# Moving three tiles' gates in between expert blocks, in a two-layer decoder step

## The chip, the cores and the metric

The kernel runs on one core of a Trainium2 chip. The metric is the time of one execution on the device, in microseconds (us). TensorE multiplies matrices into PSUM, VectorE and ScalarE work on elements, GpSimd issues the indirect transfers, SyncE issues most others, and 16 DMA engines move the data. The engines run on their own and meet at semaphores.

## The reference

One step of a two-layer decoder over 1024 prompt rows and 8 sample rows, width 1024, all float32. Each layer mixes (convolution, attention, a matrix memory), normalises to `h1`, and then computes what this case is about:

```python
def hier_moe(xf, w_group, b_group, w_expert, b_expert, e_gate, e_up, e_down):
    ...
    top_w, top_i = lax.top_k(jax.nn.softmax(e_in, axis=-1), TOP_K)      # TOP_K = 2 of 32 experts
    ...
    return grouped_experts(xf, expert_idx, top_w, e_gate, e_up, e_down)
# per expert block
        hb = jax.nn.silu(xb @ e_gate[e]) * (xb @ e_up[e])               # 1024 -> 256
        return hb @ e_down[e]                                           # 256 -> 1024
# in hybrid_layer
    ple = jnp.einsum('blp,pd->bld', p, w_pe) * jax.nn.sigmoid(jnp.einsum('bld,de->ble', h1, w_pg))
    out = layer_norm(DN_ALPHA * h1 + moe + ple, ln2_g, ln2_b)
```

## The kernel before

One function, `mix_route_experts`, runs once per layer and holds one instruction list per engine. Its order is written out by hand; nothing plans it. Rows are in 9 tiles of 128: eight of the prompt and tile 8 (`TP`), the sample's, of which 8 rows are real.

**Gates and embeddings.** For each tile, `gates(t)` multiplies `h1` by `w_pg` in two halves of 512 columns (8 chunks, 16 matmul instructions each half), `embeddings(t)` multiplies the turned `p` by `w_pe`. ScalarE takes the sigmoid of the first, VectorE multiplies and adds `ALPHA * h1`, and ScalarE stores the result to `BASE` in HBM; `sig` has two buffers, so tile t waits for the store of tile t-2. Before tile 1 the counting matmuls (L2254, L2255) feed VectorE's routing, which ends in three results: the experts' order (`turn_ready`), the row of each token (`dx_ready`), a table of leftover blocks (`r_ready` 2).

**Experts.** GpSimd scatters the rows of `h1` to `XR`, sorted by expert. The experts are ranked by their number of rows. Rank decides how many units of 32 rows an expert gets, from `TURNS`: one gets 4, 18 get 3, 13 get 2, most rows first. 84 units make 21 blocks (`QUADS`) of 4 units. Four units run side by side in TensorE, each against its own expert's weights. Block q is, on TensorE: `gate_up(q)`, `rows_turned(q + 1)`, `down(q - 1)`, `hidden_turned(q)`. So a block of 3- or 4-unit experts takes one or two new experts, and a block of 2-unit experts always two.

**Weights.** An expert's gate and up (2 MB) and down (1 MB) lie in one of five slots, expert e in slot e % 5. The slots lie over buffers that are dead by then: two in the place of `w_out`, the third over the turned `h1` (hT), the fourth over `w_pg`, the fifth ahead of `w_out`. Slots 0 and 1 are loaded during the gates, slot 2 after tile 5's gate, slots 3 and 4 when the gates, and the base's stores, are through. After that SyncE's list `todo` is sorted by the block that frees each buffer: gate and up after `gate_up` of the slot's last expert, down after its `down`. SyncE waits in that order; a request stands behind all waits before it. Up to four blocks' rows (`XSLOTS`) are in flight.

## Time and profile before

| | us |
|---|---|
| median of 3 runs | 2509.39 |
| lowest, highest | 2506.54, 2510.14 |
| the profiled execution's own time | 2510.29 |
| its span | 2508.6 |
| TensorE busy | 2261.3 (90%) |
| VectorE, ScalarE, GpSimd busy | 1158.4, 703.9, 335.8 |
| DMA | 511.92 MB, mean 204 GB/s |

The span is the part that the trace covers; some 1.7 us lie around it. Busy time is a sum over stages with different limits, so a stage is read by its own stretch: this layer's gates and experts are at 776 to 1204 us of the first layer and 1998 to 2426 of the second. In the rows, an idle time in brackets is what the engine stood still before that row, with who ended it.

### The profile page before, as it was taken

Reading aid. Unit: us, or ns where it says so; the run is one execution under the profiler, and the core shown is the slowest. Engines: PE = TensorE matmul, PEld = TensorE weight load, DVE = VectorE, ACT = ScalarE, POOL = GpSimd, SP = SyncE. Lnnn points to the kernel's source line nnn. Section 1 sums busy time; section 2 is a strip of 40 time slices with the busy share of each in tenths; the row PEclk is TensorE's granted clock in tenths of the full one; section 3 lists DMA queues with packets and bytes.
Section 4 is the critical chain, followed back from the end, with each engine's and each line's share of the span. In section 5 each row is a group of like instructions: output and inputs, shape, how many; then the busy total and the mean of one; then the engine's idle time right before and its main releaser. Section 6 shows DMA issues by size and latency. Waiting matters only on the chain. (4 is left out here: it accounts for less than half of the span.)

```text
span 2508.6 us, 39733 instructions
## 1 busy us (share of the span) xinstructions
PE 2261.3 (90%) x14448; PEld 1170.3 (47%) x14448; DVE 1158.4 (46%) x2946; ACT 703.9 (28%) x1434; POOL 335.8 (13%) x514
## 2 busy tenths in 40 slices
PE   7999968888998999988599999688889899999767
PEld 3555545566554443322255555455655444333223
DVE  3444446655877122222345554466568631322116
ACT  2555544433311010000154555444322100000012
POOL 1111008720001100000100000495000020000011
PEclk9999989989999999999799999899999999999888
DMA  9476127632412549999753321665332072799976
GB/s 345 154 278 215 60 73 206 166 92 120 161 39 96 220 163 417 420 421 421 264 174 111 99 67 54 165 179 129 120 127 99 22 282 100 308 420 420 420 289 249
DMA packets 229646, 511.92 MB, mean 204 GB/s; under 512 B 60614, under 2 KB 138382, under 8 KB 204088
## 3 DMA queue, kind: packets, MB, share of 16 engines
q1 hardware_dynamic: 182760, 385.68, 42.3%
q0 software_dynamic: 27136, 85.62, 9.6%
q10 hardware_dynamic: 19552, 38.02, 4.0%
q8 instruction: 119, 1.95, 0.3%
q14 instruction: 79, 0.65, 0.1%
HBM read 382.90 MB, written 126.32 MB: 203 GB/s over the span
## 5 line engine op out<-in xcount | busy, mean ns | idle before, releaser
L507 PE MATMUL pj_zp<-pj_w,pj_xT 128*128 128x512 f32 (+1 forms) x1280 | 503.1, 540 | 3.2 <-DMA pj_w<-in_w_in 2.3
L2270 PE MATMUL op_bank<-ex_wgu,ex_xT 128*32 128x512 f32 x2688 | 309.6, 614 | 41.1 <-DMA ex_wgu<-in_e_up 39.8
L507 PEld LDWEIGHTS pj_zp<-pj_w,pj_xT 128*128 128x128 f32 x1280 | 224.8, 191 | 201.1 <-issue 192.7
L2119 PE MATMUL op_bank<-op_wout,op_hT 128*128 128x512 f32 x512 | 227.1, 601 | 3.5 <-DVE h L2550 2.0
L2194 PE MATMUL op_bank<-op_wpg,op_hT 128*128 128x512 f32 x448 | 197.0, 598 | 0.0
L2270 PEld LDWEIGHTS op_bank<-ex_wgu,ex_xT 128*32 128x32 f32 x2688 | 87.8, 113 | 231.0 <-issue 225.4
L2771 DVE TENSOR_TENSOR ex_h<-ex_sil,op_bank 128x256 f32<-128x256 f32 x42 | 17.7, 421 | 333.9 <-ACT ex_sil L2431 333.9
L2431 ACT ACTIVATE ex_sil<-op_bank 128x256 f32<-128x256 f32 x42 | 16.1, 384 | 519.7 <-PE op_bank L2270 519.7
L2292 PE MATMUL op_bank<-ex_wd,ex_hT 128*32 128x512 f32 x1344 | 152.9, 595 | 2.5 <-DVE ex_y L2767 1.5
L2119 PEld LDWEIGHTS op_bank<-op_wout,op_hT 128*128 128x128 f32 x512 | 97.4, 193 | 121.3 <-issue 118.8
L1248 ACT ACTIVATE at_p<-at_s,at_nmx 128x640 f32<-128x640 f32 (+7 forms) x128 | 94.8, 740 | 173.4 <-DVE at_nmx L1211 172.7
L2194 PEld LDWEIGHTS op_bank<-op_wpg,op_hT 128*128 128x128 f32 x448 | 86.3, 193 | 108.3 <-issue 107.7
L1159 PE MATMUL at_tp<-ident,at_p 128*128 128x128 f32 x576 | 88.4, 281 | 35.8 <-DVE at_pT L1217 25.4
L2684 DVE TENSOR_TENSOR op_sig<-op_bank,op_sig 128x512 f32<-128x512 f32 x32 | 20.6, 686 | 188.5 <-PE op_bank L2209 188.4
L2082 POOL DMA_INDIRECT scratch_XR<-h,route_row x36 | 36.5, 1014 | 521.8 <-DVEq L2742 511.4
L1209 DVE TENSOR_REDUCE at_mx<-at_s 128x1 f32<-128x640 f32 (+7 forms) x128 | 97.0, 757 | 4.5
L1149 PE MATMUL at_s<-first_qk 96*128 96x512 f32 (+3 forms) x192 | 79.1, 528 | 20.2 <-PEq L114 20.2
L478 POOL DMA_INDIRECT pj_r<-scratch_YR,route_row x18 | 19.2, 1065 | 569.6 <-issue 387.3
L1159 PEld LDWEIGHTS at_tp<-ident,at_p 128*128 128x128 f32 x576 | 62.8, 141 | 65.9 <-issue 60.6
L950 ACT ACTIVATE pj_z<-pj_zp 128x512 f32<-128x512 f32 (+1 forms) x80 | 43.2, 540 | 176.9 <-PE pj_zp L507 176.9
L1207 DVE TENSOR_TENSOR at_s<-at_s,at_mask 128x128 f32<-128x128 f32 x128 | 38.3, 299 | 101.9 <-PE at_s L1149 100.0
L2418 ACT ACTIVATE op_sig<-op_bank 128x512 f32<-128x512 f32 x32 | 18.9, 597 | 226.9 <-PE op_bank L2194 200.3
(471 smaller groups left out, 3395.1 us busy)
## 6 DMA issues: line engine op xcount, KB each, us to landing
ex_wgu<-in_e_gate SPq DMA_DIRECT2D x64, 1024.0 KB, 19.2
ex_wgu<-in_e_up SPq DMA_DIRECT2D x64, 1024.0 KB, 22.0
ex_wd<-in_e_down SPq DMA_DIRECT2D x64, 1024.0 KB, 22.4
h<-scratch_XR SPq DMA_DIRECT2D x42, 512.0 KB, 22.3
scratch_YR<-ex_y ACTq DMA_DIRECT2D x42, 512.0 KB, 8.1
scratch_XR<-pj_zero POOLq DMA_DIRECT2D x38, 512.0 KB, 7.7
pj_w<-in_w_in SPq DMA_DIRECT2D x8, 2048.0 KB, 15.8
pc_ckv<-in_cache_ckv SPq DMA_DIRECT2D x200, 64.0 KB, 2.1
```

What stands on the lines that cost most here:

```text
L507: last = pe.matmul(zp[c % ZB][:, 0:cn], xT[:, t % 2, k, :], w[:, k, c0:c0 + cn], start=(k == 0), stop=(k == KC - 1), skip_group_check=True)
L950: act.activation(z[:, t % 2, c0:c0 + cn], zp[c % ZB][:, 0:cn], ACT.Copy).then_inc(z_ready, 1)
L1149: last = pe.matmul(scores_of(n)[:, c:min(c + 512, width)], queries(j, s)[:, qb * P:(qb + 1) * P], keys(j, s)[:, c:min(c + 512, width)], st ...
L1159: last = pe.transpose(tp[e][:, kb % 4, :], probs[small(n)][units[n][1]][:, kb, :], ident[:, :])
L1207: st.did(dve.tensor_tensor(diag, diag, mask[:, :], ALU.add))
L1209: st.did(dve.tensor_reduce(mx[:, k:k + 1], out[:, 0:(qb + 1) * P], AX.X, ALU.max))
L1248: act.activation(probs[small(n)][s][:, 0:qb + 1, :].rearrange("p b n -> p (b n)"), scores_of(n)[:, 0:(qb + 1) * P], ACT.Exp, bias=nmx[:, k ...
L2082: pool.indirect_dma_start(d["XR"], bass.IndirectOffsetOnAxis(ap=dx[0:m, k, t:t + 1], axis=0), h1[0:m, t, :], None, bounds_check=XROWS - P ...
L2119: last = pe.matmul(op[n][:, :], hT[:, t, c, :], wout[:, c, n * 512:(n + 1) * 512], start=(c == 0), stop=(c == KC - 1))
L2194: last = pe.matmul(gpair[t % 2][n][:, :], hT[:, t, c, :], wpg[:, c, n * 512:(n + 1) * 512], start=(c == 0), stop=(c == KC - 1))
L2270: last = pe.matmul(gu[q % 2][part], xT[:, q % 2, c, part], wgu[s][:, :, c, :], start=(c == 0), stop=(c == KC - 1), skip_group_check=True)
L2292: last = pe.matmul(yp[n][part, :], heT[:, q % 2, c, part], wd[s][:, c, n * 512:(n + 1) * 512], start=(c == 0), stop=(c == 1), skip_group_c ...
```

## The change

Three parts.

**1. Gates in another order.** `gates` takes a half at a time. The tiles computed ahead of the experts are `EARLY` = 0, 1, 2, 3, sample tile, 4. The second half of tile 1, its embedding and the first half of tile 2 now stand ahead of the wait for the table, and the first half of tile 1 ahead of the counting matmuls.

**2. Three tiles deferred.** Tiles 5, 6 and 7 are computed in six halves, `deferred_gate(h)` and `deferred_embedding(h)`, in one PSUM bank: half 0's gate ahead of block 0, the others at the end of blocks 0 to 4; the embeddings after `gate_up` of blocks 0 to 5. Their turned p is kept in the place of the matrix memory's state. ScalarE alternates sigmoid and silu over these blocks.

**3. Slots and experts' order.** `w_pg` and tiles 4 to 7 of hT are now live until block 5, so there are only three slots for experts 0 to 14; from expert 15 on, slots 3 and 4 join. `TURNS` is reversed: the 13 experts of 2 units come first, the one of 4 last; VectorE's comparisons turn with it and lose one instruction. Three blocks' rows are in flight, not four.

```diff
 UNIT, CAP = 32, 64
 TRIPLES = 19
 TWOS = NE - TRIPLES
-TURNS = [4] + [3] * (TRIPLES - 1) + [2] * TWOS
+TURNS = [2] * TWOS + [3] * (TRIPLES - 1) + [4]
...
-SLOTS = 5
-XSLOTS = 4
+SLOTS, FIRST_SLOTS, FIRST_TURNS = 5, 3, 15
+XSLOTS = 3
+EARLY, DEFERRED = (0, 1, 2, 3, TP, 4), (5, 6, 7)
+HALVES = 2 * len(DEFERRED)
+P_ORDER = ((0, 0), (1, 0), (2, 0), (3, 0), (0, 1), (4, 0), (1, 1), (5, 0), (2, 1))
...
+def slot_of(e):
+
+    return e % FIRST_SLOTS if e < FIRST_TURNS else (FIRST_SLOTS + e - FIRST_TURNS) % SLOTS
...
-                sp.wait_ge(g_done, 2 * 6)
+                sp.wait_ge(g_done, 2 * 4)
                 load_gate_up(2)
+                sp.wait_ge(base_ready, EARLY.index(TP) + 1)
                 load_down(2)
-                sp.wait_ge(e_done, NT)
-                load_gate_up(3)
-                load_down(3)
-                for s in range(2):
-                    sp.wait_ge(base_stored[s], 16 * (NT // 2 + 1 - s))
-                load_gate_up(4)
-                load_down(4)
-                todo = [(last_quad(e - SLOTS) + 0.5, 0, load_gate_up, e) for e in range(SLOTS, NE)]
-                todo += [(last_quad(e - SLOTS) + 1.5, 1, load_down, e) for e in range(SLOTS, NE)]
+
+                todo = []
+                for e in range(FIRST_SLOTS, NE):
+                    was = before_in_slot(e)
+                    todo.append((last_quad(was) + 0.5 if was is not None else HALVES - 0.2, 0, load_gate_up, e))
+                    todo.append((last_quad(was) + 1.5 if was is not None else HALVES + 0.8, 1, load_down, e))
                 todo += [(q - XSLOTS - 0.5, 2, load_rows, q) for q in range(XSLOTS, QUADS)]
                 for _, kind, load, n in sorted(todo, key=lambda a: a[0:2]):
...
+                    was = before_in_slot(n) if kind < 2 else None
+                    if kind == 2:
+                        sp.wait_ge(tp_done, 2 * (n - XSLOTS) + 2)
+                    elif was is None and kind == 0:
+                        sp.wait_ge(late_gate, HALVES)
+                    elif was is None:
+                        sp.wait_ge(late_emb, HALVES)
+                        for s in range(2):
+                            sp.wait_ge(base_stored[s], 16 * len(range(s, NT, 2)))
+                    elif kind == 0:
+                        sp.wait_ge(gu_done, last_quad(was) + 1)
                     else:
-                        sp.wait_ge(tp_done, 2 * (n - XSLOTS) + 2)
+                        sp.wait_ge(y_all_done, last_quad(was) + 1)
                     load(n)
...
+                def deferred_gate(h):
+                    j, n = divmod(h, 2)
+                    if h:
+                        pe.wait_ge(late_mul, h)
+                    else:
+                        pe.wait_ge(sig_done, 2 * len(EARLY) - 2)
+                    for c in range(KC):
+                        last = pe.matmul(dbank[:, :], hT[:, DEFERRED[j], c, :], wpg[:, c, n * 512:(n + 1) * 512], start=(c == 0), stop=(c == KC - 1))
+                    last.then_inc(late_gate, 1)
+
+                def deferred_embedding(h):
+                    j, n = divmod(h, 2)
+                    pe.wait_ge(late_sig, h + 1)
+                    if h == 0:
+                        pe.wait_ge(pT_ready, NT)
+                    for c in range(2):
...
+                pe.wait_ge(l_ready, NT)
+                p_turned(0)
+                p_turned(1)
+                embeddings(0)
+                gates(1, 0)
+                pe.wait_ge(r_ready, 1)
+                pe.wait_ge(pT_ready, 2)
...
+                gates(1, 1)
+                embeddings(1)
+                for i in range(2, len(EARLY)):
+                    if EARLY[i] < TP:
+                        gates(i, 0)
+                    if i == 2:
+                        pe.wait_ge(r_ready, 2)
+                    p_turned(P_ORDER.index((i, 0)))
+                    if EARLY[i] < TP:
+                        gates(i, 1)
...
+                        pe.wait_ge(sig_done, 2 * (i - 1))
+                        sample_product(gpair[i % 2][0], hT[:, TP], wpg, KC).then_inc(g_done, 2)
+                    if i >= 3:
+                        p_turned(P_ORDER.index((i - 3, 1)))
+                    embeddings(i)
+                rows_turned(0)
+                deferred_gate(0)
...
                 for q in range(QUADS):
                     gate_up(q)
+                    if q < HALVES:
+                        deferred_embedding(q)
                     if q + 1 < QUADS:
                         rows_turned(q + 1)
                     if q:
                         down(q - 1)
                     hidden_turned(q)
+                    if q + 1 < HALVES:
+                        deferred_gate(q + 1)
                 down(QUADS - 1)
...
+                for i, t in enumerate(EARLY):
+                    if i >= 2:
+                        act.wait_ge(base_stored[i % 2], 16 * (i // 2))
+                    if t < TP:
+                        sigmoid(i, 0)
+                    if i >= 2:
+                        p_copied(P_ORDER.index((i, 0)))
...
+                    if i >= 3:
+                        p_copied(P_ORDER.index((i - 3, 1)))
+                    if i:
+                        stored_base(i - 1)
+
+                def deferred_sigmoid(h):
+                    j, n = divmod(h, 2)
+                    i = len(EARLY) + j
+                    if n == 0:
+                        if j == 0:
+                            stored_base(i - 1)
+                        act.wait_ge(base_stored[i % 2], 16 * (i // 2))
+                    act.wait_ge(late_gate, h + 1)
+                    act.activation(sig[:, i % 2, n * 512:(n + 1) * 512], dbank[:, :], ACT.Sigmoid).then_inc(late_sig, 1)
 
...
                 for q in range(QUADS):
+                    if q < HALVES:
+                        deferred_sigmoid(q)
                     act.wait_ge(gu_done, q + 1)
                     act.activation(sil[:, q % 2, :], gu[q % 2][:, 0, :], ACT.Silu).then_inc(sil_done, 1)
                     if q:
                         stored_rows(q - 1)
+                    if q in range(2, HALVES + 1, 2):
+                        stored_base(len(EARLY) + q // 2 - 1)
...
+                def deferred(h):
+                    j, n = divmod(h, 2)
+                    i = len(EARLY) + j
+                    half = sig[:, i % 2, n * 512:(n + 1) * 512]
+                    dve.wait_ge(late_emb, h + 1)
+                    TT(half, dbank[:, :], half, ALU.mult).then_inc(late_mul, 1)
+                    if n == 1:
+                        dve.wait_ge(late_mul, h + 1)
+                        dve.scalar_tensor_tensor(sig[:, i % 2, :], h1[:, DEFERRED[j], :], ALPHA, sig[:, i % 2, :], ALU.mult, ALU.add).then_inc(base_ready, 1)
```

What the change moves, at three places (first layer; rows with a number of instructions are merged).

TensorE around the routing, before. `op_wpg` are gates, `op_wpe` embeddings, `ro_ones` and `ro_before` the counting matmuls, `op_p` transposes of p:

```order
L2158 MATMUL op_bank<-ident,op_p 128x128 x4
L2209 MATMUL op_bank<-op_wpe,op_pT 128x512 x4
L2254 MATMUL op_bank<-ro_OS,ro_ones 128x288
L2255 MATMUL op_bank<-ro_OS,ro_before 128x288
L2194 MATMUL op_bank<-op_wpg,op_hT 128x512 x16
L2158 MATMUL op_bank<-ident,op_p 128x128 x2
L2209 MATMUL op_bank<-op_wpe,op_pT 128x512 x4
```

and now:

```order
L2184 MATMUL op_bank<-ident,op_p 128x128 x4
L2233 MATMUL op_bank<-op_wpe,op_pT 128x512 x4
L2217 MATMUL op_bank<-op_wpg,op_hT 128x512 x8
L2288 MATMUL op_bank<-ro_OS,ro_ones 128x288
L2289 MATMUL op_bank<-ro_OS,ro_before 128x288
L2217 MATMUL op_bank<-op_wpg,op_hT 128x512 x8
L2233 MATMUL op_bank<-op_wpe,op_pT 128x512 x4
L2217 MATMUL op_bank<-op_wpg,op_hT 128x512 x8
L2184 MATMUL op_bank<-ident,op_p 128x128 x2
L2217 MATMUL op_bank<-op_wpg,op_hT 128x512 x8
L2233 MATMUL op_bank<-op_wpe,op_pT 128x512 x4
```

Half a gate went ahead of the counting matmuls, and a half, an embedding and a half ahead of the next transposes of p, which hold the wait for the table.

TensorE from the end of block 1's gate and up, before (`ex_wgu`, `ex_wd` are weights by slot, the first slot having the lowest number):

```order
L2270 MATMUL op_bank<-ex_wgu_9165,ex_xT 32x512
L2168 MATMUL op_bank<-ident,h 128x128 x8
L2292 MATMUL op_bank<-ex_wd_9168,ex_hT 32x512 x16
L2279 MATMUL op_bank<-ident,ex_h 128x128 x2
L2270 MATMUL op_bank<-ex_wgu_9165,ex_xT 32x512 x2
L2270 MATMUL op_bank<-ex_wgu_9166,ex_xT 32x512 x2
```

and now, with `op_wpe` the deferred embedding and `op_wpg` the deferred gate:

```order
L2322 MATMUL op_bank<-ex_wgu_9163,h 32x512 x2
L2252 MATMUL op_bank<-op_wpe,ms_C 128x512 x2
L2194 MATMUL op_bank<-ident,h 128x128 x8
L2342 MATMUL op_bank<-ex_wd_9168,ex_hT 32x512 x2
L2342 MATMUL op_bank<-ex_wd_9169,ex_hT 32x512 x2
...
L2329 MATMUL op_bank<-ident,ex_h 128x128 x2
L2243 MATMUL op_bank<-op_wpg,op_hT 128x512 x8
L2322 MATMUL op_bank<-ex_wgu_9164,h 32x512 x2
L2322 MATMUL op_bank<-ex_wgu_9165,h 32x512 x2
```

Each of the first blocks got a half embedding of 2 instructions and a half gate of 8 (each is two in the trace), and block 1 reads two slots in equal parts.

SyncE where slots 3 and 4 are first loaded, before (right ahead of the sorted list):

```order
L2025 DMA ex_wd_9170<-in_e_down 128x2048
...
L2019 DMA ex_wgu_9166<-in_e_gate 128x2048
L2019 DMA ex_wgu_9166<-in_e_up 128x2048
...
L2025 DMA ex_wd_9171<-in_e_down 128x2048
...
L2019 DMA ex_wgu_9167<-in_e_gate 128x2048
L2019 DMA ex_wgu_9167<-in_e_up 128x2048
...
L2025 DMA ex_wd_9172<-in_e_down 128x2048
L2013 DMA h<-scratch_XR 128x1024
```

and now (in the list, behind block 5's requests; `ex_wd_9169` is expert 13's down):

```order
L2034 DMA h<-scratch_XR 128x1024
...
L2040 DMA ex_wgu_9166<-in_e_gate 128x2048
L2040 DMA ex_wgu_9166<-in_e_up 128x2048
...
L2040 DMA ex_wgu_9167<-in_e_gate 128x2048
L2040 DMA ex_wgu_9167<-in_e_up 128x2048
...
L2040 DMA ex_wgu_9163<-in_e_gate 128x2048
L2040 DMA ex_wgu_9163<-in_e_up 128x2048
...
L2046 DMA ex_wd_9169<-in_e_down 128x2048
...
L2046 DMA ex_wd_9170<-in_e_down 128x2048
L2034 DMA h<-scratch_XR 128x1024
...
L2046 DMA ex_wd_9171<-in_e_down 128x2048
```

The two slots moved from the list's start to the middle of it, and the down weights of expert 13 stand behind three gate-and-up pairs, those of experts 15, 16 and 17.

## Rows read from the trace of the kernel before

**Rows 1.** Busy time by stretch: start:end, length, each engine's busy us, clock, DMA share, GB/s.

```profile
843.00:921.00 78.00, 78.00 (x245) 36.13 (x247) 13.64 (x17) 7.07 (x14) 0.00 (x0) 1.00 0.29 106
922.40:1204.10 281.70, 259.58 (x2222) 90.14 (x2214) 71.67 (x129) 9.34 (x22) 0.00 (x0) 0.96 0.97 398
2144.70:2426.00 281.30, 259.75 (x2223) 89.79 (x2214) 71.65 (x129) 9.34 (x22) 0.00 (x0) 0.96 0.97 398
940.00:1100.00 160.00, 160.00 (x1406) 55.37 (x1402) 44.78 (x81) 4.99 (x13) 0.00 (x0) 1.00 1.01 419
1123.80:1130.00 6.20, 6.20 (x36) 1.75 (x40) 0.00 (x0) 0.00 (x0) 0.00 (x0) 0.59 1.00 410
```

**Rows 2.** TensorE in order of time around the routing: start, length, line, idle before.

```profile
778.07 3.60 PE L2209 MATMUL op_bank<-op_wpe,op_pT 128*128 128x512 f32 x8
786.27 1.30 PE L2254 MATMUL op_bank<-ro_OS,ro_ones 128*128 128x288 f32 x2 [4.60 <-ACT op_pT L2398]
788.32 15.19 PE L2194 MATMUL op_bank<-op_wpg,op_hT 128*128 128x512 f32 x32
807.21 0.51 PE L2158 MATMUL op_bank<-ident,op_p 128*128 128x128 f32 x2 [3.69 <-DVEq L2755]
807.55 5.30 PE L2209 MATMUL op_bank<-op_wpe,op_pT 128*128 128x512 f32 x8
812.68 13.90 PE L2194 MATMUL op_bank<-op_wpg,op_hT 128*128 128x512 f32 x32
826.41 0.39 PE L2158 MATMUL op_bank<-ident,op_p 128*128 128x128 f32 x2
830.08 13.90 PE L2194 MATMUL op_bank<-op_wpg,op_hT 128*128 128x512 f32 x32
```

**Rows 3.** TensorE in order of time, a steady block and the last ones.

```profile
943.69 7.07 PE L2270 MATMUL op_bank<-ex_wgu,ex_xT 128*32 128x512 f32 x64
951.78 3.64 PE L2292 MATMUL op_bank<-ex_wd,ex_hT 128*32 128x512 f32 x32
955.79 4.50 PE L2270 MATMUL op_bank<-ex_wgu,ex_xT 128*32 128x512 f32 x40
...
1123.79 9.55 PE L2270 MATMUL op_bank<-ex_wgu,ex_xT 128*32 128x512 f32 x64 [10.22 <-DMA ex_wgu<-in_e_up]
...
1200.46 3.64 PE L2292 MATMUL op_bank<-ex_wd,ex_hT 128*32 128x512 f32 x32 [0.75 <-DVE ex_y L2767]
```

**Rows 4.** TensorE's waits in the first layer's expert blocks: us, times, longest.

```profile
PE op_bank L2270 <- DMA ex_wgu<-in_e_up: 20.2, 5, 10.2
PE op_bank L2292 <- DMA ex_wd<-in_e_down: 0.5, 1, 0.5
```

**Rows 5.** VectorE in order of time: after the counting wait, and its last table.

```profile
789.64 0.09 DVE L2697 MEMSET ro_pre<- 128x32 f32 x1
...
806.92 0.17 DVE L2754 CAST ro_tab<-ro_tabf 128x4 int32<-128x4 f32 x1
```

**Rows 6.** ScalarE in order of time: a store waited for, a table load.

```profile
822.02 0.60 ACT L2418 ACTIVATE op_sig<-op_bank 128x512 f32<-128x512 f32 x1 [13.51 <-DMA scratch_BASE<-op_sig]
...
926.88 1.28 ACT L2431 ACT_TABLE_LOAD   x1 [4.64 <-DVE op_sig L2679]
```

**Rows 7.** TensorE in order of time: rows turned, sample tile, first gate and up.

```profile
917.06 1.05 PE L2168 MATMUL op_bank<-ident,h 128*128 128x128 f32 x8
918.04 3.66 PE L2101 MATMUL op_bank<-op_wpg,op_hT 128*32 128x256 f32 x64
921.52 1.05 PE L2101 MATMUL op_bank<-op_wpe,op_pT 128*32 128x256 f32 x16
922.38 7.05 PE L2270 MATMUL op_bank<-ex_wgu,ex_xT 128*32 128x512 f32 x64
```

**Rows 8.** SyncE's loads of gate and up at 879.5, with no queue.

```profile
DMA to landing us min/median/max: 6.4/7.3/8.2
```

**Rows 9.** The page's DMA issues, one row: size and median us to landing.

```profile
ex_wgu<-in_e_up SPq DMA_DIRECT2D x64, 1024.0 KB, 22.0
```

More of the change, by code:

```diff
@@ L1816, in at, with uses_of, before_in_slot @@
         return self.nc.alloc_sbuf_tensor_at(name, shape, dt, offset=self.base + offset)
-SLOTS = 5
-XSLOTS = 4
+SLOTS, FIRST_SLOTS, FIRST_TURNS = 5, 3, 15
[5 more added lines that the diff above has]
+    return e % FIRST_SLOTS if e < FIRST_TURNS else (FIRST_SLOTS + e - FIRST_TURNS) % SLOTS
+def uses_of(e):
+    return sum(slot_of(x) == slot_of(e) for x in range(e + 1))
+def before_in_slot(e):
+    return max((x for x in range(e) if slot_of(x) == slot_of(e)), default=None)
 def first_quad(e):
@@ L1947, in mix_route_experts @@
         msp = bank[7]
-        tpe, gu, htp, yp = (four(0), four(1)), (pair(2), pair(3)), (bank[4], bank[5]), (bank[6], bank[7])
-        htp = [b[:, 0:2 * P].rearrange("p (c n) -> p c n", c=2) for b in htp]
+        tpe, gu, yp = (four(0), four(1)), (pair(2), pair(3)), (bank[6], bank[7])
+        htp = [pair(4)[:, i, :].rearrange("p (c n) -> p c n", c=2) for i in range(2)]
+        dbank = bank[5]
         c_loaded, r_loaded, wpg_loaded, p_loaded = ph.sem("c_loaded"), ph.sem("r_loaded"), ph.sem("wpg_loaded"), ph.sem2("p_loaded")
@@ L2237, in _ @@
                 logits_turned(NT - 1)
-                for t in range(NT):
-                    if t == TP:
-                        rows_turned(0)
-                    if t:
-                        gates(t)
-                    else:
-                        pe.wait_ge(l_ready, NT)
-                        p_turned(0)
-                    if t == 1:
-                        pe.wait_ge(r_ready, 2)
-                    if t + 1 < NT:
-                        p_turned(t + 1)
-                    embeddings(t)
-                    if t == 0:
-                        pe.wait_ge(r_ready, 1)
-                        pe.wait_ge(pT_ready, 2)
-                        pe.matmul(bank[6][:, 0:NT * NE], ones[:, :], OS[:, :, :].rearrange("p t e -> p (t e)"), start=True, stop=True)
-                        pe.matmul(bank[7][:, 0:NT * NE], before[:, :], OS[:, :, :].rearrange("p t e -> p (t e)"), start=True, stop=True).then_inc(r_pe, 1)
+                pe.wait_ge(l_ready, NT)
@@ L2368, in root, with load_p @@
                     act.activation(dx1[:, :], vx[:, :], ACT.Sqrt).then_inc(xd_done, 1)
-                def load_p(t):
-                    act.dma_start(pp[:, t % 2, :], of_layer(d["p_all"], layer)[rows(t)]).then_inc(p_loaded[t % 2], 16)
+                def load_p(k):
+                    i, late = P_ORDER[k]
+                    act.dma_start(pp[:, k % 2, :], of_layer(d["p_all"], layer)[rows((DEFERRED if late else EARLY)[i])]).then_inc(p_loaded[k % 2], 16)
                 y_copied(0)
@@ L2717, in _ @@
                 dve.sem_inc(turn_ready, 1)
-                do(TS(late[:, :], order[:, :], 1.0, float(TRIPLES + 1), ALU.add, ALU.min))
+                do(TS(late[:, :], order[:, :], float(TWOS), 0.0, ALU.subtract, ALU.max))
                 do(dve.scalar_tensor_tensor(tx[:, :], order[:, :], 2.0, late[:, :], ALU.mult, ALU.add))
-                do(TT(tx[:, :], tx[:, :], ty[:, :], ALU.subtract))
                 do(TS(tx[:, :], tx[:, :], float(UNIT), None, ALU.mult))
@@ L2755, in _ @@
                 dve.sem_inc(r_ready, 1)
-                for t in range(1, TP):
-                    gate(t)
+                for i in range(1, len(EARLY)):
+                    gate(i)
                 rows_turned(0)
-                gate(TP)
                 def rows_out(q):
@@ L2786, in _ @@
                     for n in range(2):
[L2787 removed]
+                        last = dve.tensor_copy(xT[0][:, 4 * n:4 * n + 4, :], tpe[n])
                     last.then_inc(rest_xT, 1)
```

190 lines of the change are left out of this document (94 added, 96 removed).

## The prediction, on record before the changed kernel ran

> **What bounds the kernel now.** Read first the busy time of each engine by stretch, then TensorE in order of time, then who it waited for. In the expert blocks of the first layer, 922.4 to 1204.1, TensorE is busy 259.6 of 281.7 us and the DMA engines 0.97 of the time at 398 GB/s; the second layer's stretch is its double, 281.3 us [rows 1]. So two resources run level. In the stretch before it, 843 to 921, they do not: TensorE is busy all 78 us while DMA is at 0.29 [rows 1]. There TensorE computes the gates, one tile in 17.4 us (812.68 to 830.08: 13.90 for the gate's 32 matmuls, 3.60 for the embedding's 8, 0.39 for two transposes) [rows 2], and hardly a weight can be fetched, since nothing frees a slot. The bill comes at the end. In blocks 0 to 15 TensorE never waits for weights (a block is 12.1 us, 943.69 to 955.79: 7.07 gate and up, 3.64 down, the rest transposes [rows 3]); in the last blocks, where each expert has two units and a block takes two new experts, it waits 20.2 us in 5 places [rows 4]. After the longest, 10.22 us, the next gate-and-up takes 9.55 us in place of 7.07, at a granted clock of 0.59 [rows 1, 3]. Without waits the stretch would be 9.2 (block 0, no down) + 19 x 12.1 + 15.4 (last gate and up, two downs, transposes) = 254.5 us; it is 281.7. So lateness costs 27.2 us a layer: 20.7 of waits on weights, the rest mostly slow clock.
>
> A second place is the routing. TensorE stands 4.60 us at 786.27 and 3.69 us at 807.21, and what follows is slow: 15.19 for 13.90, 5.30 for 3.60 [rows 2].
>
> The sum is made on the first layer and doubled, against the execution's own 2510.3 us (span 2508.6), 0.9 over the median of the three runs, 2509.4.
>
> **Part 1, the order of TensorE around the routing.** Now gates of tile 1, first half, stand before the two counting matmuls, and the second half, the embedding of tile 1 and the first half of tile 2 stand before the wait for VectorE's last table. The counting result comes at about 778.1+3.5+6.9+1.0 = 789.5; VectorE reaches its wait for it at 789.64 [rows 5], so its chain to 806.92 is not moved. TensorE from 789.5: 6.9 (half a gate) + 3.4 (embedding) + 6.9 = 806.8, against the table at 807.1. Both gaps close and nothing is slow: tile 2 ends at 807.1+0.3+6.9+3.4 = 817.7. Before it ended at 830.1 [rows 2]: 12.4 us gained.
>
> What may be late there is ScalarE. It waits for the store of the base two tiles back before each sigmoid; in the kernel before, that cost 13.51 us at 822.02 [rows 6], hidden since TensorE had a whole tile in hand. Now the copies of the turned p stand behind the same wait, and TensorE needs them sooner. The first store now goes out at about 797, ahead of the weights, and is harmless. The second goes out at about 815 into full DMA; with the 13.5 us of before it lands at 829, and TensorE wants the copy behind it at 832. The next two have margins of minus 3 to plus 3 us. Bounds 0 and 5 us a layer; I take 1, nearer to the row in which this wait was hidden.
>
> **Part 2, three tiles deferred.** Removed ahead of the experts: 3 x 17.4 = 52.2 us. Added ahead: one half gate, 6.9. So the first gate-and-up starts at 922.4 [rows 7] - 12.4 - 52.2 + 6.9 + 1 = 865.7; walked tile by tile with the sample tile's 3.66 + 1.05 [rows 7] and the extra turned-p steps it is 867.4, which I use. Its rows are there: the scatters end where they did (about 841), the three loads follow.
>
> In the blocks TensorE issues 11 pieces more: 6 half embeddings of 1.7 and 5 half gates of 6.9. Blocks 1 to 4 become 12.1+1.7+6.9 = 20.7 us, block 0 17.1, block 5 13.8, the other 14 stay 12.1, and the last with its two downs is 15.4. Together 17.1+82.8+13.8+169.4+15.4 = 298.5 us with no wait: end at 1165.9.
>
> VectorE gains a 512-column multiply per half and a 1024-column add per tile, under 2 us of a 20.7 us block in which it is mostly idle. ScalarE gains a sigmoid of 0.60 per half and, as sigmoid and silu use different tables, 10 more table loads a layer. The row shows one at 926.88, 1.28 us, finished before the silu's input was [rows 6]. Each new load has a whole gate-and-up (7 us) or half gate (6.9) over it, so I count nothing; without that cover a sigmoid would be late by 1.3. The Trainium skill (ScalarE: Activation LUTs, What ACT_TABLE_LOAD costs) puts a switch at 1.28 us plus a drain of about 1.38. By that the ten would be some 27 us of ScalarE a layer, still under the cover; the trace agrees on 1.28 and shows no drain apart.
>
> **Part 3, the weights: slots and order.** An expert is 3 MB, rows in and out 0.5 MB each. Blocks 0 to 5 take two experts each, with 3 slots: with a quarter MB of base that is 7.6 MB (decimal), 18.1 us at 419 GB/s [rows 1], inside 20.7. But the second expert of block q+1 can be asked for only when gate-and-up q is done, 13.7 us before it is needed. An unqueued pair of gate and up loads landed 6.4 to 8.2 us after issue [rows 8]. So blocks 1 to 5 do not wait. Before block 6 there is no half gate to cover, only 7.0 us: a wait of about 1.
>
> Block 6's down, run in turn 7, is the weak place. Expert 13's down weights may only be asked for after down 5, and SyncE's queue, which is in order, by then holds gate and up of experts 13, 14, 15, 16 and 17. Count from the end of gate-and-up 5 (974): 5 pairs of 2.1 MB, three downs of 1.05, one of rows, two stores and one base: 15.7 MB, 37.4 us at 419, landing at about 1012. TensorE wants it 7.0+12.1+7.0+1.1 = 27.2 us after 974, at 1001. A wait of about 11 us, and 2.5 of slow clock behind it, as after 10.22 before [rows 3]. The waits sum to 14.5 a layer. From there on the blocks take 4/3 of an expert, 5.2 MB or 12.5 us of DMA per 12.1 of TensorE, but five slots are ahead, and the stream is through before TensorE: 77 MB from 974 take 184 us, to 1158. No wait follows, and the last blocks, 3 units each, do not starve.
>
> The Trainium skill (DMA: Bandwidth & Descriptors, Specifications) names an HBM limit of about 358 GB/s per core. By it blocks 1 to 5 would need 21.2 us of DMA against 20.7, and the stream after 974 would be through at 1189 in place of 1158, past the end forecast below. The trace's 419 over 160 us [rows 1] says otherwise, and the sum goes by the trace.
>
> **Sum.** End of the experts at 1165.9+14.5 = 1180.4, before 1204.1 (1200.46 + 3.64 [rows 3]): 23.7 us a layer, 47.4 in both. 2510.3 - 47.4 = 2462.9, and 0.9 less for the median: 2462. What follows the blocks (last store, barrier, gather) is the same work.
>
> **Rivals.**
> - The block-7 wait is small, because SyncE's requests drain sooner than counted or the downs come in time. For: in the kernel before, the loads' lead absorbed every such burst up to block 15. Against: the order above is fixed. It gives 2462 - 2 x 13 = 2436.
> - The early gain fails: ScalarE's base stores, or p loads stuck in the scatter's traffic (stores 13.5 us [rows 6]), hold TensorE up to 8 us a layer, or the table wait at 807 stays. 2462 + 16 = 2478. For: four of those waits now have margins under 3 us. Against: the first store leaves before the weights.
> - The change does not do what it says: DMA, idle for some 20 us from 855 until the first gate-and-up ends, with only 3 slots, is the bound, and what was saved early comes back as waits later, so only the routing gain stays: 2510 - 25 = 2485. Against: the 77 MB count above.
> - Slower: the three slots are too few. The place is the wait for gate and up in blocks 1 to 6, the price is landing time minus 13.7 us in five blocks and minus 7.0 in the sixth. It decides from the landing time at which 6L - 75.5 exceeds 23.7, 16.5 us. At 22.0, the median of all the up loads [rows 9], it is 56.5 us a layer, and the kernel ends at 2462 + 113 = 2575. For: that median. Against: it was queued time with five slots' requests in line, where here the queue drains before each new burst.
>
> **How the numbers follow.** Forecast 0.62, small wait 0.12, early gain lost 0.13, DMA bound 0.07, slower 0.05, and 0.01 that it nets to nothing. Two runs of this kernel differ by up to 0.15%, so 0.2% (5 us) is what can be told from none. The first four are faster: 0.94; within 0.2%: 0.02; slower: 0.04 (a mild case of the last rival still wins). The range takes the first rival to two thirds and the second whole: 2442 to 2480.
>
> **What would show it.** The counting matmuls start near 788.6 and tile 1's second half follows without a gap; the first gate-and-up at 866 to 869 and a distance of 20.7 us between blocks 1 to 5; ten more table loads a layer with no TensorE wait that names ScalarE; one wait on the down weights in turn 7, 9 to 13 us, followed by slow matmuls; none in blocks 15 to 20; the end near 1180. Waits at every block 1 to 5 would show the last rival, a first gate-and-up later than 872 the second. I am wrong if the time leaves 2442 to 2480.

## The result, and the profile after

| | before | after |
|---|---|---|
| median (runs) | 2509.76 us (4) | 2474.05 us (4) |
| lowest, highest | 2506.54, 2510.41 | 2469.27, 2477.28 |
| ratio, 95% interval | | 0.9858, 0.9846 to 0.9870 |
| profiled run, its span | 2510.29, 2508.6 | 2473.88, 2472.2 |
| TensorE, VectorE, ScalarE busy | 2261.3, 1158.4, 703.9 | 2248.4, 1158.0, 729.2 |
| DMA | 511.92 MB, 204 GB/s | 511.91 MB, 207 GB/s |

The kernel gains 35.7 us where 47.4 was predicted. The time lies in the range of 2442 to 2480. Of e9's six runs below, five took 2492.37 to 2493.87 us and one, a slow run that is left out of its ratio, 6019.73 us. The same bytes are moved and TensorE's work is the same; what shrinks is its idle time and its time at the lower clock.

Spans of two executions differ a little ahead of the change too, so each layer is measured from its first transposes of p to the end of its last down:

| layer | before | after | gain |
|---|---|---|---|
| first | 776.31 to 1204.10 = 427.8 | 779.56 to 1190.14 = 410.6 | 17.2 |
| second | 1998.58 to 2425.99 = 427.4 | 1981.33 to 2391.54 = 410.2 | 17.2 |

The clock of the first layer thus starts 3.25 us later after the change, and that has to be taken off before times of the two are compared. Together the two layers gain 34.4 us of the 36.4 between the spans. The forecast was 23.7 a layer: 6.5 are missing in each.

**The routing.** TensorE after the change, in order of time: start, length, operation, and in brackets the idle time before it.

```profile
784.76 7.03 PE L2217 MATMUL op_bank<-op_wpg,op_hT 128*128 128x512 f32 x16
791.62 0.65 PE L2288 MATMUL op_bank<-ro_OS,ro_ones 128*128 128x288 f32 x2
...
792.59 7.03 PE L2217 MATMUL op_bank<-op_wpg,op_hT 128*128 128x512 f32 x16
799.46 3.60 PE L2233 MATMUL op_bank<-op_wpe,op_pT 128*128 128x512 f32 x8
802.89 7.03 PE L2217 MATMUL op_bank<-op_wpg,op_hT 128*128 128x512 f32 x16
810.22 0.51 PE L2184 MATMUL op_bank<-ident,op_p 128*128 128x128 f32 x2 [0.30 <-DVEq L2844]
...
817.43 3.60 PE L2233 MATMUL op_bank<-op_wpe,op_pT 128*128 128x512 f32 x8
...
845.28 0.47 PE L2184 MATMUL op_bank<-ident,op_p 128*128 128x128 f32 x2 [2.81 <-ACT op_pT L2456]
845.69 1.34 PE L2127 MATMUL op_bank<-op_wpe,op_pT 128*32 128x256 f32 x16
846.96 8.51 PE L2217 MATMUL op_bank<-op_wpg,op_hT 128*128 128x512 f32 x16
...
873.91 7.07 PE L2322 MATMUL op_bank<-ex_wgu,h 128*32 128x512 f32 x64
```

The gaps of 4.60 and 3.69 us of [rows 2] are down to nothing and 0.30, and no matmul there runs slow. VectorE's table, which ends the second wait, comes 30.7 us after the first transposes of p (810.22 - 779.56), before 30.9 (807.21 - 776.31): its chain did not move. Tile 2 ends 41.3 us after the transposes (820.86, where the next gate starts), before 53.8 (830.08): 12.5 gained. The first gate-and-up comes at 873.91, 870.7 on before's clock. Ahead of it there is a new wait of 2.81 us for ScalarE at 845.28, and behind it half a gate takes 8.51 in place of 7.03 us and the sample's embedding 1.34 in place of 1.05 [rows 7]. What ScalarE did, in order of time:

```profile
835.66 1.17 ACTq L2467 DMA_DIRECT2D scratch_BASE<-op_sig  x1
844.38 0.33 ACTq L2426 DMA_DIRECT2D op_p<-in_p_all  x1
844.76 0.38 ACT L2456 ACTIVATE op_pT<-op_bank 128x256 f32<-128x256 f32 x1 [8.74 <-DMA scratch_BASE<-op_sig]
...
874.70 1.28 ACT L2508 ACT_TABLE_LOAD   x1
```

It stood 8.74 us for a base store issued at 835.66 (tile 2's, two tiles back), with the copy of the sample's turned p behind that wait. In the second layer the same wait holds TensorE 3.71 us. The extra table loads are there, ten a layer; none holds TensorE up.

**The blocks.** TensorE in block 1, block 6, turn 7 and at the last down:

```profile
890.83 7.07 PE L2322 MATMUL op_bank<-ex_wgu,h 128*32 128x512 f32 x64
897.83 1.98 PE L2252 MATMUL op_bank<-op_wpe,ms_C 128*128 128x512 f32 x4
...
900.62 3.64 PE L2342 MATMUL op_bank<-ex_wd,ex_hT 128*32 128x512 f32 x32
...
904.54 7.03 PE L2243 MATMUL op_bank<-op_wpg,op_hT 128*128 128x512 f32 x16
...
989.92 8.64 PE L2322 MATMUL op_bank<-ex_wgu,h 128*32 128x512 f32 x64 [2.52 <-DMA ex_wgu<-in_e_up]
...
1024.00 5.23 PE L2342 MATMUL op_bank<-ex_wd,ex_hT 128*32 128x512 f32 x32 [12.25 <-DMA ex_wd<-in_e_down]
...
1186.50 3.64 PE L2342 MATMUL op_bank<-ex_wd,ex_hT 128*32 128x512 f32 x32 [0.75 <-DVE h L2855]
```

Blocks 1 to 5 start at 890.83, 911.50, 932.18, 952.85 and 973.52, without a wait. Then two waits for weights in the first layer, and none in blocks 8 to 20, where before there were six in the last blocks [rows 4]. In the second layer they are 1.56 (block 6), 1.96 and 9.93 us (downs). SyncE's requests in between, in order of time:

```profile
981.79 1.42 SPq L2040 DMA_DIRECT2D ex_wgu<-in_e_up  x1
...
984.40 0.44 SPq L2040 DMA_DIRECT2D ex_wgu<-in_e_up  x1
...
991.05 0.41 SPq L2040 DMA_DIRECT2D ex_wgu<-in_e_up  x1
...
992.77 0.39 SPq L2040 DMA_DIRECT2D ex_wgu<-in_e_up  x1
...
999.76 0.38 SPq L2040 DMA_DIRECT2D ex_wgu<-in_e_up  x1
1004.00 1.43 SPq L2046 DMA_DIRECT2D ex_wd<-in_e_down  x2
```

The first row is the up of expert 13, which block 6 waited for; it landed 8.0 us after its issue. The second is the up of expert 14, which only block 7 reads.

The down weights wanted at 1011.75 were asked for at 1004.00, right behind the down that frees their buffer, and were there at 1024.0. The ups of experts 15, 16 and 17 (991.05, 992.77, 999.76) had gone ahead of them, each with its gate. The engines by stretch, columns as in [rows 1]:

```profile
873.90:980.50 106.60, 106.60 (x663) 40.11 (x662) 20.98 (x35) 19.61 (x22) 0.00 (x0) 1.00 0.83 326
980.50:1190.00 209.50, 193.97 (x1664) 66.98 (x1660) 54.59 (x97) 6.14 (x16) 0.00 (x0) 0.96 0.91 371
980.60:1024.00 43.40, 28.63 (x224) 10.46 (x225) 10.11 (x17) 1.15 (x3) 0.00 (x0) 0.84 0.99 396
1010.00:1020.00 10.00, 1.75 (x16) 0.97 (x8) 1.62 (x3) 0.38 (x1) 0.00 (x0) 0.68 1.02 424
1050.00:1150.00 100.00, 100.00 (x880) 34.37 (x872) 28.20 (x51) 3.07 (x8) 0.00 (x0) 1.00 1.02 420
```

In blocks 0 to 5 TensorE never stands and DMA has room (0.83). While TensorE waits at 1010 to 1020, the DMA engines run at their full 424 GB/s.

### The profile page after: what moved, and what is told of

Its sections match the earlier page's. It is cut to its first block and busy times, and to the rows that moved or that the text cites. A ratio compares the mean times of both kernels' runs of the same rounds, so it can differ in the third digit from the quotient of the medians.

```text
span 2472.2 us, 39715 instructions
## 1 busy us (share of the span) xinstructions
PE 2248.4 (91%) x14448; PEld 1161.8 (47%) x14448; DVE 1158.0 (47%) x2944; ACT 729.2 (29%) x1454; POOL 335.9 (14%) x514
## 2 busy tenths in 40 slices
DMA packets 229645, 511.91 MB, mean 207 GB/s; under 512 B 60614, under 2 KB 138382, under 8 KB 204088
## 5 line engine op out<-in xcount | busy, mean ns | idle before, releaser
L2322 PE MATMUL op_bank<-ex_wgu,h 128*32 128x512 f32 x2688 | 298.7, 596 | 4.1 <-DMA ex_wgu<-in_e_up 4.1
L2342 PE MATMUL op_bank<-ex_wd,ex_hT 128*32 128x512 f32 x1344 | 157.7, 611 | 25.6 <-DMA ex_wd<-in_e_down 24.1
L2322 PEld LDWEIGHTS op_bank<-ex_wgu,h 128*32 128x32 f32 x2688 | 83.9, 110 | 193.6 <-issue 190.2
L2342 PEld LDWEIGHTS op_bank<-ex_wd,ex_hT 128*32 128x32 f32 x1344 | 41.1, 112 | 110.7 <-issue 104.7
L2217 PEld LDWEIGHTS op_bank<-op_wpg,op_hT 128*128 128x128 f32 x256 | 48.8, 193 | 59.1 <-issue 58.9
## 6 DMA issues: line engine op xcount, KB each, us to landing
ex_wgu<-in_e_gate SPq DMA_DIRECT2D x64, 1024.0 KB, 13.0
ex_wgu<-in_e_up SPq DMA_DIRECT2D x64, 1024.0 KB, 15.3
ex_wd<-in_e_down SPq DMA_DIRECT2D x64, 1024.0 KB, 14.6
```

What stands on the lines that cost most here:

```text
L2217: last = pe.matmul(gpair[i % 2][n][:, :], hT[:, t, c, :], wpg[:, c, n * 512:(n + 1) * 512], start=(c == 0), stop=(c == KC - 1))
L2322: last = pe.matmul(gu[q % 2][part], xT[q % 2][:, c, part], wgu[s][:, :, c, :], start=(c == 0), stop=(c == KC - 1), skip_group_check=True)
L2342: last = pe.matmul(yp[n][part, :], heT[:, q % 2, c, part], wd[s][:, c, n * 512:(n + 1) * 512], start=(c == 0), stop=(c == 1), skip_group_c ...
```

## The experiments

Each was timed beside the kernel before; ratios are to it. Lengths "of the stage" are from the first transposes of p to the end of the last down, both layers added: before 855.2, after 820.8.

### Was ScalarE's store wait worth what it seemed? (e1_copy_first)

The changed kernel, with the copy of the sample's turned p ahead of the wait for the store. That copy doesn't touch the stored buffer.

```diff
                 for i, t in enumerate(EARLY):
+                    if t == TP:
+                        p_copied(P_ORDER.index((i, 0)))
                     if i >= 2:
                         act.wait_ge(base_stored[i % 2], 16 * (i // 2))
                     if t < TP:
                         sigmoid(i, 0)
-                    if i >= 2:
+                    if i >= 2 and t < TP:
                         p_copied(P_ORDER.index((i, 0)))
```

> The changed kernel with one edit: for the sample tile ScalarE copies the turned p before it waits for the store of the base two tiles back, not behind that wait. Theory (the early gain was cut by that store, which lands late in the scatter's traffic, and the copy stood behind it): TensorE's wait of 2.8 and 3.7 us before the second transposes of the sample tile goes, and the slow clock behind it too, some 4.5 us a layer, 9 us in all: about 2465 us. Rival (the p loads or the store itself bound that place): the wait moves to the sample tile's embedding or to tile 4 and the time stays at 2474.

Measured: 2464.13 us (2463.19 to 2466.79), ratio 0.9827 (0.9815 to 0.9840), 10 us under the changed kernel. In TensorE's order of time the wait and the slow half gate are gone:

```profile
838.89 0.51 PE L2184 MATMUL op_bank<-ident,op_p 128*128 128x128 f32 x2
...
840.33 7.13 PE L2217 MATMUL op_bank<-op_wpg,op_hT 128*128 128x512 f32 x16
```

The first gate-and-up comes 89.9 us after the transposes of p, in place of 94.4; the later waits keep their lengths nearly (2.8 at block 6, 12.1 at turn 7). So it is shown that the copy's place causes this wait, and that the wait costs 4.5 us a layer where it stands. By the stage the layers gain 3.9 and 4.1 us: some 0.5 us of each is given back later.

### Is the long wait the order of the requests or the stream? (e2_slots_last, e3_interleaved)

e2: the gate and up of experts 15 and 16 are asked for behind the down weights of 13 and 14. e3: the two kinds alternate. Each has its own line `moved`, shown here as a comment.

```diff
                 todo += [(q - XSLOTS - 0.5, 2, load_rows, q) for q in range(XSLOTS, QUADS)]
+                # e2: moved = {(0, 15): 6.6, (0, 16): 6.6}
+                # e3: moved = {(1, 13): 6.1, (0, 16): 6.2, (1, 14): 6.3, (0, 17): 6.4}
+                todo = [(moved.get((kind, n), key), kind, load, n) for key, kind, load, n in todo]
```

> The changed kernel with SyncE's requests for gate and up of experts 15 and 16 moved behind the down weights of 13 and 14 and behind the row load of block 10. Theory (all of this stretch is one stream at 420 GB/s, so order only moves the wait): the 12.3 us wait on the down weights in turn 7 shrinks to under 1, and block 8 waits some 9 to 11 us for gate and up instead; total 2470 to 2482 us. Rival (only the order of the queue is at fault, the stream has room): the wait goes and nothing takes its place, 2474 - 27 = 2447.

Measured: 2478.67 us (2475.88 to 2479.76), ratio 0.9877 (0.9863 to 0.9892). TensorE in order of time:

```profile
1011.62 3.64 PE L2344 MATMUL op_bank<-ex_wd,ex_hT 128*32 128x512 f32 x32 [0.95 <-DMA ex_wd<-in_e_down]
...
1027.69 9.94 PE L2324 MATMUL op_bank<-ex_wgu,h 128*32 128x512 f32 x64 [11.99 <-DMA ex_wgu<-in_e_up]
```

The wait of 12.25 us shrinks to 0.95, and 11.99 stands one step later, with 2.87 of slow matmuls in place of 1.59. The order decides who waits, not how much has to be moved.

> The changed kernel with SyncE's requests interleaved by when they are needed: gate and up 15, down 13, gate and up 16, down 14, gate and up 17. Theory (one stream, each request 2.5 or 5 us of it, so requests in order of need cost least): down 13 lands about when turn 7 wants it, gate and up 16 some 2 us late for block 8; of the 13.9 us a layer 8 to 12 are gained, 2474 - 20 = 2454 us, between 2448 and 2460. Rival (the stream is short by the whole wait, as the stretch's bytes are the same): a wait of 8 us or more comes up in block 8 to 10, and the time stays above 2466.

Measured: 2464.14 us (2462.92 to 2466.84), ratio 0.9827 (0.9815 to 0.9840): a gain of 10 us on the changed kernel, where 20 were expected. TensorE's waits, both layers: us, times, longest.

```profile
PE op_bank L2324 <- DMA ex_wgu<-in_e_up: 7.5, 4, 2.1
PE op_bank L2196 <- DMA h<-scratch_XR: 5.9, 8, 1.8
PE op_bank L2344 <- DMA ex_wd<-in_e_down: 3.6, 2, 2.3
```

The waits for weights fall from 28.2 us (24.1 and 4.1) to 11.1, and the rows, which nothing waited for in the changed kernel, are late in 8 places of blocks 13 to 20. The expectation failed in its size: about half of the 20 us came. The likely reason is the stream, which it left out: once TensorE runs earlier, DMA at 420 GB/s is just behind it. e3 alone doesn't show this.

### Do the experts' order and the deferral need each other? (e4_most_first, e5_order_alone)

e4 is the changed kernel with the experts of most rows first, as before. With that order slots 3 and 4 join at expert 10, not at 15. VectorE's comparisons are turned back with it.

```diff
-TURNS = [2] * TWOS + [3] * (TRIPLES - 1) + [4]
+TURNS = [4] + [3] * (TRIPLES - 1) + [2] * TWOS
...
-SLOTS, FIRST_SLOTS, FIRST_TURNS = 5, 3, 15
+SLOTS, FIRST_SLOTS, FIRST_TURNS = 5, 3, 10
```

> The changed kernel with the experts' order put back to most rows first (the slots change over at expert 10 in place of 15, since the first blocks then take fewer experts). Theory (the order is what lets the deferral pay: the long first blocks must be the ones that take two experts): the first blocks of 20.7 us take 4/3 experts and leave DMA idle, and the last, two experts in 12.1 us, wait as before, 15 to 20 us a layer; 2500 us, between 2490 and 2510. Rival (the deferral alone brings the gain by giving DMA time): within 10 us of the changed kernel.

Measured: 2507.24 us (2502.32 to 2509.72, 12 runs), ratio 0.9996 (0.9987 to 1.0004): no difference from before. TensorE's waits, both layers:

```profile
PE op_bank L2322 <- DMA ex_wgu<-in_e_up: 37.3, 14, 4.8
PE op_bank L2342 <- DMA ex_wd<-in_e_down: 9.3, 4, 5.4
```

In the first layer 15.2 us of them fall in the last blocks (from 1116 us on), as expected. The other 6.9 us stand at 997 to 1031, where slots 3 and 4 first join, so not all of e4's loss is the starving end.

e5 is the kernel before with few rows first, and nothing else (VectorE's comparisons turned with it, as in the change).

```diff
-TURNS = [4] + [3] * (TRIPLES - 1) + [2] * TWOS
+TURNS = [2] * TWOS + [3] * (TRIPLES - 1) + [4]
```

> The kernel before with the experts' order reversed and nothing else. Theory (the order pays only with long first blocks): the first blocks take two new experts in 12.1 us while slots 3 and 4 have only begun to fill, so the waits move from the last blocks to blocks 2 to 7, 20 to 28 us a layer with slow clock behind the long ones: 2508.8 plus 0 to 20, most likely 2520 us. Rival (few rows first is better by itself, since the end no longer starves): 2500 us or less.

Measured: 2522.19 us (2518.66 to 2526.07), ratio 1.0047 (1.0033 to 1.0061), slower by 13. The waits for weights are 44.0 and 7.2 us where before they were 39.8 and 1.0: they have moved to the front blocks (935 to 1048 us in the first layer), where two new experts a block meet 12.1 us of TensorE. So the order alone loses, and the deferral without it gives back all that the rest of the change saves. Two parts of the change, three slots in place of five at first and three blocks' rows in flight in place of four, were not varied by themselves.

### What is the routing's part? (e6_routing_alone, e9_routing_undone)

e6 is the kernel before with part 1 only. Its core:

```diff
                     embeddings(t)
                     if t == 0:
+                        gates(1, (0,))
                         pe.wait_ge(r_ready, 1)
...
+                    if t == 2:
+                        gates(2, (0,))
+                        pe.wait_ge(r_ready, 2)
+                        p_turned(2)
+                        gates(2, (1,))
+                    elif t == 1:
+                        gates(1, (1,))
```

> The kernel before with the first part of the change alone: half gates and the embedding of tile 1 ahead of the counting matmuls and of the wait for the table; nothing deferred, slots and experts' order as before. Theory (TensorE bounds this stage, and the experts begin as much earlier as it is done): both gaps close, the first gate and up starts 12.4 us earlier and so does the end of the stream, 25 us in both layers: 2508.8 - 25 = 2484 us. Rival (the stream of weights sets the end, the earlier start is waited away in the last blocks): more than 22 us a layer of waits on weights, and less than half of the gain.

Measured: 2480.09 us (2476.76 to 2482.25), ratio 0.9888 (0.9873 to 0.9903). The stage is 829.0 us, 26.2 less than before; the first gate-and-up comes 134.1 us after the transposes of p in place of 146.1, and the waits for weights stay as they were (40.0 us in 10 places, longest 10.2).

e9 is the changed kernel with part 1 undone. ScalarE's copies of the turned p go back with TensorE's order, which the cut doesn't show.

```diff
-                gates(1, 0)
                 pe.wait_ge(r_ready, 1)
...
+                gates(1, 0)
                 gates(1, 1)
+                pe.wait_ge(r_ready, 2)
+                p_turned(2)
                 embeddings(1)
```

> The changed kernel with its first part undone: the counting matmuls and the wait for the table come where they were before, deferral, slots and experts' order stay. Theory A (the parts meet at the sample tile: its store wait exists only because TensorE comes there before the scatters end, so 12 us later it does not wait): about 24 us slower for the two gaps, 9 us given back, 2474 + 15 = 2489. Rival B (the parts simply add): 2474 + 25 to 29 = 2499 to 2503.

Measured: 2493.4 us (2492.37 to 2493.87 in five of six runs), ratio 0.9933 (0.9920 to 0.9946), 19 over the changed kernel. The number falls between the theories. TensorE's waits in the first layer ahead of the blocks show why:

```profile
PE op_bank L2287 <- ACT op_pT L2457: 4.6, 1, 4.6
PE op_bank L2184 <- ACT op_pT L2457: 3.6, 2, 2.6
PE op_bank L2184 <- DVEq L2848: 3.3, 1, 3.3
```

Both gaps are back (4.6 and 3.3), but the store wait did not leave (2.6): the store is late too. ScalarE issues it at 844.17 and stands 8.55 us for it, where in the changed kernel it issues at 835.66 and stands 8.74. Theory A's reason thus falls. The stage is 843.2 us: part 1 is worth 26.2 on the kernel before and 22.4 on top of the rest, parts 2 and 3 are worth 12.0 without it and 8.2 with it. Of the 3.8 between, 1.5 stand ahead of the first gate-and-up, which part 1 brings forward by 24.0 us in both layers without the rest and by 22.5 on top of it. The other 2.3 come behind it and were not traced to one wait.

### Both mended, and two tries at the rest (e7_both_mended, e8_rows_ahead, e10_halves_later)

e7 is e1's and e3's edits together.

> The changed kernel with both mends: the sample tile's copy ahead of the store wait, and SyncE's requests interleaved. Theory: the first brings experts and stream alike 4.5 us forward, the second takes waits out of the blocks, so they add: 2474 - 10 - 10 = 2454 us. Rival (with the waits on order gone, the stream is the bound and swallows the earlier start): 2460 to 2464, with more waits in blocks 13 to 20.

Measured: 2453.09 us (2449.19 to 2453.85), ratio 0.9774 (0.9761 to 0.9787). It is 21 us under the changed kernel and 56 under the one before; only e8 is as fast. TensorE from block 6 on, waits for weights split into small ones:

```profile
983.39 7.08 PE L2324 MATMUL op_bank<-ex_wgu,h 128*32 128x512 f32 x64 [1.67 <-DMA ex_wgu<-in_e_up]
...
992.71 3.64 PE L2344 MATMUL op_bank<-ex_wd,ex_hT 128*32 128x512 f32 x32 [1.15 <-DMA ex_wd<-in_e_down]
...
1006.92 3.64 PE L2344 MATMUL op_bank<-ex_wd,ex_hT 128*32 128x512 f32 x32 [2.05 <-DMA ex_wd<-in_e_down]
...
1012.62 7.07 PE L2324 MATMUL op_bank<-ex_wgu,h 128*32 128x512 f32 x64 [1.62 <-DMA ex_wgu<-in_e_up]
```

Four waits, 6.5 us in sum, and not one slow matmul behind them in this layer. The second layer has three such waits, of 1.57, 2.06 and 2.40 us, and behind the last two the matmuls take 5.34 in place of 3.64 and 8.77 in place of 7.07. So small waits can spare the time at the lower clock, but need not.

e8 is e7 with a block's rows asked for ahead of down weights of the same place in the list.

```diff
+                rank = (0, 2, 1)
-                for _, kind, load, n in sorted(todo, key=lambda a: a[0:2]):
+                for _, kind, load, n in sorted(todo, key=lambda a: (a[0], rank[a[1]])):
```

> The kernel with both mends, and with each block's row load asked for ahead of the down weights of the same block, not behind them. Theory (rows in blocks 13 to 20 came 0.3 to 1.8 us late, 5.9 us in both layers, since they stood behind two downs, 5 us of stream): those waits go, 4 to 6 us under the kernel with both mends, 2449 us. Rival (the stream is the bound there, so the wait only changes its name, from rows to weights): no difference.

Measured: 2453.25 us (2451.00 to 2455.40), ratio 0.9778 (0.9765 to 0.9792): no difference from e7. The waits for rows vanish (5.7 us before), those for gate and up rise from 7.3 to 11.6. All waits on DMA together go from 18.3 to 16.3 us, and the slow matmuls behind block 6's and 8's waits from 3.4 to 5.1, so the trade is nearly even. It fits the rival, the stream as the bound, but part of it came in blocks 6 to 8, ahead of the rows that were moved.

e10 is e7 with every deferred half a block later, so that half a gate covers block 6's loads. ScalarE's and VectorE's parts move with it.

```diff
                 rows_turned(0)
-                deferred_gate(0)
...
-                    if q < HALVES:
-                        deferred_embedding(q)
+                    if 1 <= q <= HALVES:
+                        deferred_embedding(q - 1)
...
-                    if q + 1 < HALVES:
-                        deferred_gate(q + 1)
+                    if q < HALVES:
+                        deferred_gate(q)
```

> The kernel with both mends, and with every deferred half one block later: no gate ahead of block 0, gates at the end of blocks 0 to 5, embeddings behind gate and up of blocks 1 to 6. Theory (the stream of weights starts when the first gate and up ends, DMA is idle before that, and block 6 waits since no half gate stands before it): the stream starts 7 us earlier, block 6 gets 6.9 us of cover, and the waits of 2 us in blocks 6 to 8 go; the same work on TensorE, 5 us less of waits and slow clock a layer: 2453 - 10 = 2443 us, 2440 to 2448. Rival (TensorE's own work is the bound after the two mends): 2453.

Measured: 2458.03 us (2456.94 to 2458.77), ratio 0.9792 (0.9780 to 0.9805), 5 slower than e7 where 10 faster was expected. In the first layer the waits of blocks 6 and 7 are gone as meant (the first one left is 1.08 us at 1013.05, block 8), but there are new ones at blocks 0 and 1. TensorE:

```profile
864.59 8.77 PE L2323 MATMUL op_bank<-ex_wgu,h 128*32 128x512 f32 x64 [3.06 <-DVE h L2785]
...
882.63 7.07 PE L2323 MATMUL op_bank<-ex_wgu,h 128*32 128x512 f32 x64 [0.93 <-DMA ex_wgu<-in_e_up]
```

and VectorE ahead of the first:

```profile
860.68 1.29 DVE L2767 TENSOR_TENSOR op_sig<-op_bank,op_sig 128x512 f32<-128x512 f32 x2 [12.93 <-PE op_bank L2235]
862.11 1.23 DVE L2770 SCALAR_TENSOR_TENSOR op_sig<-h,op_sig 128x1024 f32<-128x1024 f32 x1
863.26 1.28 DVE L2785 COPY h<-op_bank 128x512 f32<-128x512 f32 x2
```

The half gate ahead of block 0 had covered VectorE's multiply, add and copy of the rows; without it the rows come 3.06 us late, and the matmuls behind run slow, 8.77 for 7.07. In both layers that is 9.5 us, against 7.2 us less of waits for weights (5.4 in place of 12.6) and 1.4 more for rows (7.1 in place of 5.7). So the move fails mainly by block 0's lost cover, which the expectation had left out. The stage is 2.3 us longer than e7's; the rest of the 5 lies outside it.

## Why the prediction was right, and what was off in it

**The routing: right.** Both gaps closed, 12.5 us gained where 12.4 was worked out, and VectorE's chain stayed. e6 shows it by itself: 12.0 us a layer at the first gate-and-up (146.1 to 134.1).

**ScalarE's store wait: found and named, and sized too small.** Bounds 0 and 5, taken at 1 because the wait was hidden before [rows 6]. Measured: 2.81 us of idle, 1.5 of slow gate and 0.3 of slow embedding, 4.6; e1 gives 4.5. The term should have counted the clock behind a wait as well, as was done for the long one. That is 3.5 of the 6.5 us missing a layer. It is also why the first gate-and-up came at 870.7 on before's clock, outside the 866 to 869 named as a sign and short of the 872 that would have shown the second rival: that rival came true by half. With it gone, the first gate-and-up is at 89.9 us after the transposes of p, and the walk (867.4 less its 1, from 776.31) gives 90.1. The "margins of minus 3 to plus 3" held at their lower end, and the later stores were not the ones that counted.

**Blocks 0 to 5: right.** 20.7 us a block, no wait, ten table loads hidden. The rival of too few slots, 2575, is out: gate and up loads in blocks 1 to 5 landed 4.8 to 11.9 us after issue, median 8.1, nearer to [rows 8] than to the 22.0 of [rows 9]. The remark that the queue drains before each burst was the right one. By the 358 GB/s of the Trainium skill (DMA: Bandwidth & Descriptors, Specifications) these blocks would have needed an estimated 21.2 us of DMA each and waited; the trace disagrees, with 420 GB/s over 100 us later on.

**Block 6: the second mis-sized term.** Taken at 1 us; it waits 2.52 and then runs 8.64 for 7.07, 4.1 in all: 3.1 of the missing 6.5. The 1 us fits the slowest landing of [rows 8], 8.2 us, less the 7.0 us of cover. The landing was right: expert 13's up, which the trace names as what TensorE waited for, took 8.0 us. Two terms were left out. The up was issued only at 981.79, 1.2 us after the gate-and-up that frees its buffer had ended (980.59), since the wait and the gate's issue come first. And the 1.6 us of slow matmuls behind the wait were not counted at all.

**Turn 7: right in place and cause, in size partly by luck.** 12.25 us plus 1.59 slow, 13.8, against 11 plus 2.5, 13.5. Counted from the end of gate-and-up 5, the down weights landed after 43.4 us (980.59 to 1024.0), not 37.4, and TensorE wanted them after 31.2, not 27.2; the two misses nearly cancel. The 4.0 are block 6's lateness. The 6.0 are more bytes, 17.2 MB at 396 GB/s against the 15.7 MB counted at 419. That is about the down and the rows asked for right behind (1005.1 and 1005.47), which the count leaves out; that these are the bytes is not shown. The cause is shown in both its halves: the order of the requests put the wait there (e2 moves it one step on), and the bytes asked for ahead are what it lasts for, at a full DMA (424 GB/s). That it could be cut to a few us by alternating (e3) was not foreseen.

**No waits from block 9 on: right.** The first layer's stage ends at 1190.14, which is 1186.9 on before's clock, against 1180.4 forecast. The 6.5 us are the store wait and block 6 above, 3.5 and 3.1; turn 7 adds 0.3, and some 0.4 less elsewhere was not traced.

**The parts.** The prediction gave the routing 25 us and the rest 22 of the 47. Measured by the stage it is 22 to 26 for the routing and 8 to 12 for the rest. Where the deferral's gain went can be added up: lateness cost 27.2 us a layer before, and of that 13.8 came back at turn 7, 4.1 at block 6 and 4.6 at the store wait. It leaves 4.7 in the first layer, 9.4 if both are alike, inside the 8 to 12.

## What to carry to other kernels

Work moved into a memory-bound stretch helps as far as the transfers can use the time it makes; count bytes per step on both sides, and choose the order of the steps so that those that need the most bytes stand beside the moved work. Price a new wait with the slow matmuls that may follow it, and from the issue of the load, not from the moment its buffer is free. Before moving work away from a place, look what it covered there. Where one queue serves several buffers, alternate the requests in the order in which they are wanted, and put no copy behind a wait for a store that it doesn't need.
